# Residual norms of a decoder layer: where the gate, the norm weight and the modulation are applied, and by which engine

## The reference, cut to what matters

```python
mod = (jax.nn.silu(c) @ w_ada + b_ada)[:, None, :]
sh1, sc1, gt1, sh2, sc2, gt2 = jnp.split(mod, N_MOD, axis=-1)
h = rmsnorm(x, g_pre_mix) * (1.0 + sc1) + sh1
m, k_rows, v_rows, s_new = token_mixer(h, w_in, ..., w_out, ...)
x = x + gt1 * rmsnorm(m, g_post_mix)
h = rmsnorm(x, g_pre_ffn) * (1.0 + sc2) + sh2
f = (jax.nn.silu(h @ w_ffn_gate) * (h @ w_ffn_up)) @ w_ffn_down
x = x + gt2 * rmsnorm(f, g_post_ffn)
```

## Time and profile before

| | |
|---|---|
| median of 3 runs | 1586.3 us (1580.81, 1586.3, 1587.44) |
| the profiled execution | 1587.41 us, its span 1585.8 us |
| PE busy | 1475.4 us (93%), mean granted clock 0.956 |
| DVE, ACT, POOL busy | 933.2, 643.8, 103.2 us |
| output projection to first FFN matmul | about 739.3 to 781.0 us of the span |
| last down matmul to the end | about 1559.4 to 1585.8 us |

### The profile page before, as it was taken

How to read it: one execution, slowest core, us unless ns; L and a number is a source line. 1 busy time by engine, 2 the same in 40 slices (tenths; PEclk the granted TensorE clock), 3 DMA queues, 4 the chain that set the end, 5 groups by cost and what they waited for, 6 DMA issues and landing times.

```text
span 1585.8 us, 28737 instructions
## 1 busy us (share of the span) xinstructions
PE 1475.4 (93%) x11316; PEld 1297.0 (82%) x11316; DVE 933.2 (59%) x1025; ACT 643.8 (41%) x1211; POOL 103.2 (7%) x192
## 2 busy tenths in 40 slices
PE   5859998996889998999799999999999999999996
PEld 2227787885668777886499999999999999999995
DVE  1343599995678654435756566666656664445445
ACT  0024377675544543332234434334443433334332
POOL 0000311112323210000000000000000000000000
PEclk7869999998989998999799999999999999999999
DMA  9989999999889964799655665565556556555551
GB/s 357 386 330 341 368 361 399 346 332 371 307 297 362 339 210 160 294 348 348 248 171 176 183 184 175 172 188 181 174 183 185 174 171 191 179 180 180 182 161 55
DMA packets 138271, 394.43 MB, mean 249 GB/s; under 512 B 12874, under 2 KB 17137, under 8 KB 125377
## 3 DMA queue, kind: packets, MB, share of 16 engines
q1 hardware_dynamic: 117730, 319.39, 59.5%
q0 software_dynamic: 20464, 74.00, 12.2%
HBM read 382.14 MB, written 11.21 MB: 248 GB/s over the span
## 4 chain that ended last, share of the span: by engine, by line
PE 75%; DVE 9%; DMA 9%; issue 3%; ACT 2%; SPq 1%; POOLq 0%; POOL 0%; ACTq 0%; DVEq 0%
PE ps L1655 22%; PE ps L1656 21%; PE ps L1657 21%; PE ps L1588 4%; DVE k_page L1145 3%; DMA ada_s<-in_w_ada 2%; DMA k_page<-in_cache_k 2%; PE ps L1787 2%; DVE w_lo L1097 2%; DMA ada_r<-in_w_ada 1%; DMA vec_rows<-in_g_gla_out 1%; PE ps L1618 1%; DMA x_keep<-x_t 1%; ACT k_page L732 1%; DMA raw<-in_w_in 1%
## 5 line engine op out<-in xcount | busy, mean ns | idle before, releaser
L1655 PE MATMUL ps<-h_hi,w_hi 128*128 128x264 f32 x2304 | 671.8, 292 | 17.6 <-DVE h_lo L1063 15.4
L1656 PE MATMUL ps<-h_lo,w_hi 128*128 128x264 f32 x2304 | 661.7, 287 | 0.0
L1657 PE MATMUL ps<-h_hi,w_lo 128*128 128x264 f32 x2304 | 660.9, 287 | 0.0
L1655 PEld LDWEIGHTS ps<-h_hi,w_hi 128*128 128x128 f32 x2304 | 441.6, 192 | 67.4 <-issue 54.0
L1529 DVE TENSOR_TENSOR w_lo<-raw,w_hi 128x1024 fp32r<-128x1024 f32 x260 | 314.7, 1214 | 295.2 <-ACT w_hi L940 294.1
L940 ACT ACTIVATE w_hi<-raw 128x1024 fp32r<-128x1024 f32 x264 | 278.1, 1059 | 404.7 <-PE ps L1657 404.7
L1656 PEld LDWEIGHTS ps<-h_lo,w_hi 128*128 128x128 f32 x2304 | 441.0, 191 | 0.1
L1657 PEld LDWEIGHTS ps<-h_hi,w_lo 128*128 128x128 f32 x2304 | 439.5, 191 | 0.0
L1097 DVE TENSOR_TENSOR w_lo<-raw,w_hi 128x1024 fp32r<-128x1024 f32 x132 | 160.9, 1221 | 207.4 <-ACT w_hi L655 207.2
L655 ACT ACTIVATE w_hi<-raw 128x1024 fp32r<-128x1024 f32 x128 | 135.0, 1055 | 261.1 <-PE ps L1657 211.0
L1656 PE MATMUL ps<-act_lo,w_hi 128*128 (+1 forms) x704 | 200.4, 285 | 0.0
(11 more groups left out here) (302 smaller groups left out, 1153.1 us busy)
## 6 DMA issues: line engine op xcount, KB each, us to landing
ada_r<-in_w_ada SPq DMA_DIRECT2D x64, 1024.0 KB, 8.7
raw<-in_w_in SPq DMA_DIRECT2D x96, 512.0 KB, 6.8
raw<-in_w_ffn_gate SPq DMA_DIRECT2D x88, 512.0 KB, 3.6
raw<-in_w_ffn_up SPq DMA_DIRECT2D x88, 512.0 KB, 3.7
raw<-in_w_ffn_down SPq DMA_DIRECT2D x88, 512.0 KB, 4.6
ada_s<-in_w_ada SPq DMA_DIRECT2D x32, 1024.0 KB, 11.0
k_page<-in_cache_k POOLq DMA_DIRECT2D x64, 512.0 KB, 7.4
v_page<-in_cache_v POOLq DMA_DIRECT2D x38, 512.0 KB, 7.0
```

The lines of the kernel that those rows point to most:

```text
L1655: mm(out, w_hi, xh, start=first, stop=False)
L1656: mm(out, w_hi, xl, start=False, stop=False)
L1657: return mm(out, w_lo, xh, start=False, stop=last)
```

## The change

Six parts, in the order of the program:

- **Ada steps earlier.** Steps 32 to 47 stand every 5/4 slots instead of every 3/2, 48 to 51 at slots 123 to 126, their transposition at 121 instead of 125. SP issues loads 48 to 52 at slots 118 to 123; 53 to 59 behind the first four FFN units and 60 to 63 between the next four. After slot 127 PE makes step 52, the branch sum, 53 to 55, and then each quarter's sum comes before its step and not behind it.
- **Branch squares and gate during the projection.** `MIX_AT` has slots 105, 113 and 121: DVE squares a finished group of four chunks there, and one slot later multiplies the group by gate times norm weight (`gated`: four `tensor_scalar` with a per-partition factor and one small product) and adds up the squares. The reciprocal root commutes with this factor. The last group follows behind slot 127, its `gated` between its squares and the root.
- **The residual quarter** (`add_quarter`) is then a product with the root and one addition, both over the whole quarter.
- **FFN scale and shift on ACT.** As each quarter of `x` is there, ACT squares it and multiplies it by the scale (`x_scale`, four activations with a per-partition scale); when the second root is there DVE multiplies by it, and ACT adds the shift (four activations with a per-partition bias) and rounds.
- **First `LO` on POOL.** The four subtractions of `first_ffn_units` are made by POOL.
- **The same at the end.** The first 8 chunks of the down projection are squared and gated behind the first half, the last 8 behind the second, and the last residual is `add_quarter`.

```diff
-        A_SLOT.update({32 + k: 102 + 3 * k // 2 for k in range(16)})
+        A_SLOT.update({32 + k: 102 + 5 * k // 4 for k in range(16)})
+        A_SLOT.update({48 + k: 123 + k for k in range(4)})
-        TURN_AT = {20: 2, 55: 3, 125: 4}
+        TURN_AT = {20: 2, 55: 3, 121: 4}
+        MIX_AT = {8 * (NIN + 1 + gi) + 1: gi for gi in range(NOUT - 1)}
...
+                    if 48 <= n < 53 and s == (118, 119, 122, 123, 123)[n - 48]:
+                        if n == 48:
+                            sp.wait_ge(vtok_out, 32)
+                            sp.wait_ge(rows_out, 64)
                         ada_load(n)
...
-            for n in range(48, 64):
+            for n in range(53, 60):
                 ada_load(n)
             for u in range(4, UPC):
                 w_unit(wg_v, 0, u, W_FFN + u - 3)
+                ada_load(56 + u)
...
+            pool.wait_ge(lo_ready, W_FFN)
+            for u in range(4):
+                pool.wait_ge(hi_ready, W_FFN + u + 1)
+                g.tensor_tensor(LO[:, u, :], RAW[:, u, :], HI[:, u, :].bitcast(F32), ALU.subtract).then_inc(lo_ready, 1)
...
+            def x_scale(q):
+                act.wait_ge(scl_ready, 1)
+                for k in range(4 * q, 4 * q + 4):
+                    ins = s.activation(F_LO[:, k, 0:TP], X[:, k, 0:TP], ACT.Identity, scale=scale_t[:, k, 0:1])
+                ins.then_inc(x_scaled, 1)
...
-            h_high(4)
+            for q in range(4):
+                act.wait_ge(h32_ready, 4 + q + 1)
+                for k in range(4 * q, 4 * q + 4):
+                    ins = s.activation(F_LO[:, k, 0:TP], F_LO[:, k, 0:TP], ACT.Identity, bias=MOD[:, 3 * KC + k, 0:1])
+                link(ins)
+                s.activation(H_HI[:, 4 * q:4 * q + 4, :], F_LO[:, 4 * q:4 * q + 4, :], ACT.Copy).then_inc(hhi_ready, 1)
...
+                if st in MIX_AT:
+                    c = MT * MIX_AT[st]
+                    dve.wait_ge(bank_out, MT * NIN + c + MT)
+                    link(v.tensor_tensor(SQD[:, c:c + MT, :], MT_[:, c:c + MT, :], MT_[:, c:c + MT, :], ALU.mult))
+                if st - 1 in MIX_AT:
+                    c = MT * MIX_AT[st - 1]
+                    link(gated(MT_, c, c + MT))
+                    if c:
+                        link(v.tensor_tensor(SQD[:, 0:MT, :], SQD[:, 0:MT, :], SQD[:, c:c + MT, :], ALU.add))
+                if st == 123:
+                    fold(SQD, MT)
...
+            def gated(src, k0, k1):
+                for k in range(k0, k1):
+                    v.tensor_scalar(src[:, k, 0:TP], src[:, k, 0:TP], scale_t[:, k, 0:1], None, ALU.mult)
+                return v.tensor_tensor(src[:, k0:k1, TP:T], src[:, k0:k1, TP:T], scale_t[:, k0:k1, 1:NC], ALU.mult)
...
+            def add_quarter(src, old, q, nx):
+                cs = slice(4 * q, 4 * q + 4)
+                link(v.tensor_tensor(src[:, cs, :], src[:, cs, :], rstd[:, :].unsqueeze(1).to_broadcast([P, 4, T]), ALU.mult))
+                v.tensor_tensor(X[:, cs, :], src[:, cs, :], old[:, cs, :], ALU.add).then_inc(x_new, 1)
+                dve.wait_ge(x_new, nx + q + 1)
...
-            for n in range(48, 52):
+            ada_next(52)
+            late_sums(SQD, 4, KC - MT)
+            for n in range(53, 56):
                 ada_next(n)
-            late_sums(SQD, 4, KC - MT)
-            for n in range(52, 56):
-                ada_next(n)
-            sums(SQD, 7, 6, sums_done, lambda q: ada_next(56 + q))
+            sums(SQD, 7, 6, sums_done, after=lambda q: ada_next(56 + q))
```

More of the change, by code:

```diff
@@ L398, in _ @@
                 w_load(s + 4)
-                for n in range(4, 48):
+                for n in range(4, 53):
                     if n < 16 and s == A_SLOT[n - 4] + 4:
@@ L947, in _ @@
                 s.activation(SQD[:, 4 * q:4 * q + 4, :], X[:, 4 * q:4 * q + 4, :], ACT.Square).then_inc(sq_ready, 1)
+                if q < 3:
+                    x_scale(q)
             rs(rstd[:, :], rvar[:, :], 5)
+            x_scale(3)
             def glu_exp(g):
@@ L1297, in hx_low, with slot @@
                     .then_inc(mix_ready, 1)
-            for st in range(NSLOT):
+            def slot(st):
                 if st + 3 < NSLOT:
@@ L1475, in early_squares @@
                 ins.then_inc(sq_ready, 1)
[L1477 to L1501, removed]
@@ new lines, in _ @@
+            for st in range(NSLOT):
+                slot(st)
+            dve.wait_ge(bank_out, MT * (NIN + NOUT))
+            v.tensor_tensor(SQD[:, KC - MT:KC, :], MT_[:, KC - MT:KC, :], MT_[:, KC - MT:KC, :], ALU.mult).then_inc(sq_ready, 1)
+            dve.wait_ge(sq_ready, 6)
+            link(gated(MT_, KC - MT, KC))
+            dve.wait_ge(mod_done, 5)
+            gain = vec2[:, V2["pre_ffn"]:V2["pre_ffn"] + KC]
+            v.scalar_tensor_tensor(scale_t[:, :, :], MOD[:, 4 * KC:5 * KC, :], 1.0, gain.unsqueeze(2).to_broadcast([P, KC, NC]),
+                                   ALU.add, ALU.mult).then_inc(scl_ready, 1)
@@ L1512, in _ @@
+            dve.wait_ge(sums_done, 2)
+            rstd_of(rstd[:, :], rvar[:, :], ps[:, 6, 0:T], D, 4)
+            dve.wait_ge(x_back, 16)
+            dve.wait_ge(scl_ready, 1)
+            for q in range(4):
+                cs = slice(4 * q, 4 * q + 4)
+                add_quarter(MT_, XOLD, q, 0)
+                link(v.tensor_tensor(F_LO[:, cs, TP:T], X[:, cs, TP:T], scale_t[:, cs, 1:NC], ALU.mult))
             dve.wait_ge(sums_done, 3)
             rstd_of(rstd[:, :], rvar[:, :], ps[:, 7, 0:T], D, 5)
-            build_h(3 * KC, 4)
+            for q in range(4):
+                cs = slice(4 * q, 4 * q + 4)
+                dve.wait_ge(x_scaled, q + 1)
+                link(v.tensor_tensor(F_LO[:, cs, :], F_LO[:, cs, :], rstd[:, :].unsqueeze(1).to_broadcast([P, 4, T]), ALU.mult))
+                v.tensor_tensor(F_LO[:, cs, TP:T], F_LO[:, cs, TP:T], MOD[:, 3 * KC + 4 * q:3 * KC + 4 * q + 4, 1:NC],
+                                ALU.add).then_inc(h32_ready, 1)
+                if q >= 1:
+                    low_h(4, q - 1)
@@ L1516, in glu_gate @@
+            low_h(4, 3)
             def glu_gate(g, nb):
@@ L1570, in _ @@
                     lo_n(j * 4 + W_DOWN, u)
-            dve.wait_ge(mod_done, 6)
-            add_norm(F_HI, X, vec2[:, V2["post_ffn"]:V2["post_ffn"] + KC], 5 * KC, F_LO, KC // 2, 4,
-                     4 * (NIN + NOUT) + KC, 6, 4)
+            for c in range(KC // 2, KC, 4):
+                dve.wait_ge(bank_out, MT * (NIN + NOUT) + c + 4)
+                v.tensor_tensor(F_LO[:, c:c + 4, :], F_HI[:, c:c + 4, :], F_HI[:, c:c + 4, :], ALU.mult).then_inc(sq_ready, 1)
+            dve.wait_ge(sq_ready, 13)
+            link(gated(F_HI, KC // 2, KC))
+            dve.wait_ge(sums_done, 4)
+            rstd_of(rstd[:, :], rvar[:, :], ps[:, 6, 0:T], D, 6)
+            for q in range(4):
+                add_quarter(F_HI, X, q, 4)
         @block.tensor
@@ L1610, in mod_turn, with sums @@
                 ins.then_inc(modt, 1)
-            def sums(src, bank, n0, done, step=None):
+            def sums(src, bank, n0, done, step=None, after=None):
                 for q in range(4):
@@ L1618, in sums @@
                         ins = mm(ps[:, bank, 0:T], ones[:, :], src[:, k, :], start=(k == 0), stop=(k == KC - 1))
-                ins.then_inc(done, 1)
+                    if q == 3:
+                        ins.then_inc(done, 1)
+                    if after is not None:
+                        after(q)
             def late_sums(src, n0, early):
```

47 lines of the change are left out of this document (24 added, 23 removed).

## The result

The changed kernel took 1595.45 us in the median of 8 runs (1588.5 to 1598.72), the kernel before 1584.91 (8 runs, 1580.04 to 1591.4): a ratio of 1.0062 (95% interval 1.004 to 1.0085), slower by some 10 us, where no change that can be told was forecast and the range ended at 1592.5. The profiled execution of the changed kernel took 1588.5, only 1.1 more than the one of before (1587.41), and was the fastest of its eight. So two questions: where the 10 us are lost, and why the profiled execution doesn't seem to show them.

What follows compares the result with a forecast made beforehand. PE fills the output projection and FFN, so the change moves only the joints between them and behind the down projection: +3.5 + 0.3 - 3.0 = +0.8 on 1587.4, 1588.2; for the median 1587.0, range 1579.5 to 1592.5.

Steps and rivals of the forecast that it cites:

- Step 1: Output projection: four more ada steps +4.8, step 47's load 1.1 late (bounds 0 and 9.2); its end moves by +5.9.
- late load: Rival, output projection: at 354 GB/s step 47's load comes 9.2 us late in place of 1.1; 1595.1 us, chance 0.09.
- step 3: Before the branch root: POOL's four subtractions, 1.91 us each, hold up DVE; +5.5 us (bounds 0 and 6.9).
- Step 2: Projection's last result (745.7) to branch root: squares, sum and root, ready at 752.7 if nothing is in the way.
- four in a row: Rival, before the branch root: POOL's four subtractions run without a break; +6.9 us, 1588.4 us, chance 0.15.
- The turns: Before the branch root: POOL takes each gap between DVE's linked instructions, `gated`'s four passing in one turn; chance 0.40.
- The first to issue holds: Rule cited for POOL against DVE: the first to issue holds the shared SBUF ports for its whole instruction.
- Steps 4 and 5: Branch root to first FFN matmul: quarters every 2.8 us, `x_scale` 1.6, last sum 775.7, matmul at 784.5, +3.5.
- Steps 6 and 7: Middle of down projection: `LO` 3.3 us later, PE waits +0.3; end: shorter residual quarters -3.0, `gated` of last chunks fits.
- The base: Profiled execution of the kernel before lies 1.1 over the runs' median, 1586.3; so 1588.2 becomes 1587.0 for the median.

Runs made afterwards that it cites:

- e7: The changed kernel again, unchanged, for a second profile: 1597.83 us (one run).
- e6: The changed kernel with loads 48 and 49 issued at slots 121 and 122, behind load 47, in place of 118 and 119: 1589.03 us, ratio 1.0023.
- e2: The changed kernel with the four first weight halves on DVE, in its wait for the second sum, in place of POOL: 1585.39 us, ratio 0.9996.
- e3: The changed kernel with the old adaLN schedule and the four first weight halves on DVE in its wait for the second sum: 1583.96 us, ratio 0.9989.
- e5: An edit of e3: PE's adaLN steps moved into its pauses, two of DVE's four weight halves behind parts of `H_LO`: 1570.21 us, ratio 0.9893.
- e1: The changed kernel with its adaLN schedule as before, the rest as changed: 1583.95 us, ratio 0.9986.
- e4: The kernel before with the new adaLN schedule alone: 1592.06 us, ratio 1.0049.
- e9: The kernel before with only e5's order of PE's steps and its placing of DVE's four weight halves: 1578.92 us, ratio 0.9943.
- e11: e5 again, unchanged, for a second profile: 1573.11 us, ratio 0.991.
- e10: The changed kernel with the old adaLN schedule and POOL's four subtractions held back into DVE's second wait: 1584.39 us (one run).

## Why the prediction was wrong

- **Step 1 failed**, in the words "At 420 it just fits; with its latency and the bursts I put it 1.1 us late". The projection grew by 12.0 and 13.3 for 5.9 forecast. The 4.8 for four steps held. The 1.1 for late loads was a wait of 4.35 and 5.38, and the low clock behind the waits added 2.6 and 2.9, a cost that the step had at nothing.
  - Its rate was too high. From 649 to 715 in the first profile, the same stretch allowing for its early start, the DMAs moved 391 GB/s (412 over 700 to 711, but 329 over 680 to 690), and from 656 to 722 in e7 372, not 420 throughout. By these 25.2 MB take 64.5 and 67.7 us of the 62, 2.5 and 5.7 late.
  - But a sum of bytes was the wrong question for the dearest wait. e6 moved 381 GB/s over 656 to 722, less than the first profile, and step 47 doesn't wait in it, since two loads that are wanted later are no longer ahead of its own. And the step asked only about step 47, where two earlier steps waited too.
  - The rival "late load" gave 1595.1, and the median was 1595.45. Its sign came true, PE idle for `ada_r` at slot 120. That its number fits to 0.4 us is luck: it had 8.1 us more in step 1 than the forecast, where 6.1 and 7.4 were measured, and step 3 made up most of the rest. At 0.09 it was much too low for a sum that "just fits".
  - The Trainium skill, SBUF — State Buffer, Summary: rules for kernel authors, has some 358 GB/s to estimate transfers from HBM; by that estimate the load would be 8.4 late. The measured 391 and 372 lie above it, but the rule would have been the better warning.
- **Step 2 held.** Unblocked, the root stands 6.54 behind the last result (e2), forecast 7.0.
- **Step 3 had the mechanism, but its price was too low.** The hold is 7.7 us (14.21 less 6.54) for 5.5 forecast and 6.9 in the rival "four in a row". What was mis-sized is a subtraction: 2.38 us, not 1.91. Four times the difference is 1.9 of the missing 2.2. The Trainium skill, GPSIMD Engine Reference, section 3.1, has 4497 ns for 2048 elements; half of it, 2.25 us, is an estimate, and the measurement is nearer to that.
  - The turns were wrong as well. POOL's four are in a row, as in that rival, and yet DVE gets in at each change; and a turn lets in one instruction, not all four of `gated`. So four short instructions beside four long ones cost all four.
  - "The first to issue holds" doesn't fit all of the earlier trace rows: in the second pair DVE's record starts 0.21 us ahead of POOL's (480.20, 480.41), and DVE is the one that is held.
- **Steps 4 and 5 held.** The quarters of `x` come every 2.81 us, `x_scale` takes 1.69 for 1.6; from the root to the FFN it is 26.30 and 25.58 for 26.3.
- **Steps 6 and 7 held.** From the FFN on -3.1 and -1.9 for -2.7. At the second down half the `LO` come 2.5 us later in their stage (1445.12 less 1438.40, less the 4.2 by which the FFN starts later), 3.3 forecast, and PE doesn't wait for them, so the +0.3 was nothing. `gated` of the last eight chunks fits ahead of the sum, for which DVE still waits 0.78. The tail's quarters are 3.0 shorter.
- **The sum.** Forecast +0.8; step 1 adds 6.1 (7.4 in e7), steps 2 and 3 together 1.7, the rest -0.4 (+0.1): 8.2 and 10.0.
- **The base.** "That execution lies 1.1 over the median" took an offset of one execution as if a second would share it. Step 32 stood from 638.8 to 650.6 in the thirteen profiles of this study, at 645.1 in the mean, so one span against another says nothing about 8 us; only stages do.

Open is why e3's median lies 4 us over what its two profiles' stages and the mean start give (933.5 + 645.1, and 1.6 that a run has over its span, are 1580.2). e5's lies 4 us under the same sum. For the changed kernel, e1, e2, e4, e6, e9 and e11 the sum is within 2 us of the median. Both undone (e3) and the schedule alone undone (e1) are apart by 2.6 us in the stages and by nothing in the runs; an interval of 3 us either way doesn't settle it. Not tried are the parts of the change that stayed in e3 one by one, and e5's new order of PE without its placing of DVE's weight halves.

## What to carry to other kernels

When loads are moved ahead, each is a delay to those behind it: list them by the time at which they are wanted, and look for one that is wanted sooner than another ahead of it. A sum of bytes over the whole stage doesn't show that. Work that one engine does for another belongs where neither waits. In the kernel before DVE idled 7.01 us in its wait for the second sum, and PE 10.35 ahead of the first FFN matmul; filling those two with work that stood on the path gave 6.7 us with nothing of the change (e9), and 12.5 together with the change's good part (e5). Compare two traces by the stages from a common instruction, and take a second profile of the same kernel before an offset is believed.

## What the runs showed of the hardware

- POOL and DVE on SBUF take turns by instruction. Beside POOL's `tensor_tensor` of 1024 elements (2.38 to 2.42 us each) DVE's `tensor_scalar` of 256 elements took 2.34 to 2.47 us for the 0.28 that it takes alone (1.14 / 4 in e2), one for each of POOL's. A DVE instruction that reads PSUM took its usual 0.43 beside POOL in e10, one case.
- The first 130 us come in two kinds, whichever the kernel: in five of the thirteen profiles the DMAs moved 378 to 382 GB/s over the first 100 us and the first adaLN step stood at 129.4 to 132.3; in eight they moved 357 to 363 and it stood at 135.6 to 137.9. From there to step 32 it took 507.6 to 513.9. Both kinds occur among e1 to e4, which ran on one chip. What sets the rate wasn't tried.
- A short wait in the middle of a busy stage can cost more than itself, since the granted clock may fall to the lower of its two levels behind it. After the wait of 2.93 us PE's matmuls came every 0.22 us in place of 0.12 until 720.5, 2.6 us in all. Waits of 2.22 and 2.42 (e7) and 3.40 (e2) cost 1.5, 1.4 and 1.5 more, and one of 2.68 (e4) nothing more, with a granted clock of 1.00. So the length of the wait alone doesn't decide it.
